# A fused transformer program on one core: first layer rebuilt up to its feed-forward

## The reference, cut to what matters

```
mod = silu(c) @ ada_w[0] + ada_b[0];  mod_c = silu(c_ctx) @ ada_w[0] + ada_b[0]
hx = rms_norm(x, norm1_g[0]) * (1 + sc1) + sh1        # and hc from ctx with mod_c
q, k, v = split(h @ attn_w_in)      # 16 query heads, 4 key and value heads of 64
q, k = rms_norm(q, q_gain), rms_norm(k, k_gain)       # per head; rope for x only
x tokens: softmax over 256 windowed keys, 256 context keys and a sink; context: 256 and a sink
x = x + g1 * (o @ attn_w_out);  hx2 = rms_norm(x, norm2_g[0]) * (1 + sc2) + sh2
x = x + g2 * conv_glu(hx2, ffn_w_up, ffn_conv_w, ffn_conv_b, ffn_w_down)
```

## Time and profile before

| | us |
|---|---|
| median of 3 executions | 2844.99 (2839.59 to 2847.72) |
| profiled execution | 2848.02, span 2846.2, mean granted clock 0.936 |
| TensorE busy over the span | 2477.9 (87%) |
| VectorE, ScalarE busy | 974.3 (34%), 775.1 (27%) |
| start to first projection | 72.5 |
| projections, then head norms to first scores | 75.4, 52 |
| attention loop with 16 modulation blocks | 197 |
| turn and output projection, entry of the feed-forward | 63, 35 |

### The profile page before, as it was taken

How to read it: one execution, slowest core, us unless ns; L and a number is a source line. 1 busy time by engine, 2 the same in 40 slices (tenths; PEclk the granted TensorE clock), 3 DMA queues, 4 the chain that set the end, 5 groups by cost and what they waited for, 6 DMA issues and landing times.

```text
span 2846.2 us, 31745 instructions
## 1 busy us (share of the span) xinstructions
PE 2477.9 (87%) x12956; PEld 1613.8 (57%) x12956; DVE 974.3 (34%) x1419; ACT 775.1 (27%) x1248; POOL 4.2 (0%) x6
## 2 busy tenths in 40 slices
PE   4939886999997997757999989799999999999995
PEld 2726653778785897654988986343333333334332
DVE  1274423334414238773654343341111111111112
ACT  2223533223314245433543453111111111111110
POOL 0000000000000000000000000000000000000000
PEclk8968997999997999887999997989999999999998
DMA  8103540442222140021555430569999999999993
GB/s 305 60 30 119 206 149 30 163 147 90 89 74 89 60 148 1 1 89 60 178 181 201 168 104 1 204 267 428 428 429 429 428 421 422 429 429 417 421 429 161
DMA packets 141897, 603.55 MB, mean 212 GB/s; under 512 B 6272, under 2 KB 51584, under 8 KB 117088
## 3 DMA queue, kind: packets, MB, share of 16 engines
q1 hardware_dynamic: 141792, 602.10, 53.5%
HBM read 601.03 MB, written 1.05 MB: 212 GB/s over the span
## 4 chain that ended last, share of the span: by engine, by line
PE 73%; DMA 10%; DVE 8%; ACT 6%; issue 2%; SPq 1%; ACTq 0%; DVEq 0%
PE bank L841 70%; DMA arena<-in_b_up 10%; ACT hT L1362 1%; PE bank L912 1%; DVE arena L2022 1%; ACT modp L1362 1%; ACT arena L1399 1%; DMA ring<-in_ada_w 1%; ACT arena L1387 1%; DVE xn L1742 1%; PE bank L873 0%; ACT modp L1338 0%; ACT hT L1376 0%; DVE modp L2012 0%; DVE xn L2011 0%
## 5 line engine op out<-in xcount | busy, mean ns | idle before, releaser
L841 PE MATMUL bank<-arena 128*64 128x512 f32 (+5 forms) x3088 | 644.2, 488 | 77.6 <-ACT arena L1692 25.7
L841 PEld LDWEIGHTS bank<-arena 128*64 128x64 f32 (+2 forms) x3088 | 340.5, 175 | 337.2 <-issue 267.5
L841 PE MATMUL bank<-ring,arena 128*64 128x512 f32 (+1 forms) x1632 | 394.9, 608 | 23.8 <-DMA arena<-in_b_up 21.0
L841 PE MATMUL bank<-hT_high,w_split 128*128 128x512 f32 (+1 forms) x1408 | 351.1, 341 | 30.4 <-issue 30.4
L841 PEld LDWEIGHTS bank<-ring,arena 128*64 128x64 f32 (+1 forms) x1632 | 141.3, 143 | 269.6 <-issue 259.7
L841 PEld LDWEIGHTS bank<-hT_high,w_split 128*128 128x128 f32 x1408 | 245.2, 192 | 60.6 <-issue 32.6
L841 PE MATMUL bank<-hT_low,w_split 128*128 128x512 f32 (+1 forms) x704 | 238.5, 339 | 0.0
L2159 DVE TENSOR_SCALAR arena<-bank 128x512 f32<-128x512 f32 x32 | 22.1, 692 | 549.5 <-PE bank L841 549.5
L841 PE MATMUL bank<-ring,hT 128*128 128x512 f32 (+1 forms) x432 | 182.6, 584 | 17.7 <-ACTq L666 17.7
L841 PEld LDWEIGHTS bank<-ring,hT 128*128 128x128 f32 x432 | 81.4, 195 | 116.6 <-issue 97.2
L841 PEld LDWEIGHTS bank<-hT_low,w_split 128*128 128x128 f32 x704 | 135.4, 192 | 15.3 <-issue 1.5
(11 more groups left out here) (307 smaller groups left out, 3418.6 us busy)
## 6 DMA issues: line engine op xcount, KB each, us to landing
ring<-in_w_gate SPq DMA_DIRECT2D x64, 2048.0 KB
arena<-in_w_down SPq DMA_DIRECT2D x64, 2048.0 KB, 15.1
ring<-in_w_up SPq DMA_DIRECT2D x32, 2048.0 KB
arena<-in_w_up SPq DMA_DIRECT2D x32, 2048.0 KB
ring<-in_ada_w SPq DMA_DIRECT2D x24, 2048.0 KB, 7.9
ring<-in_ffn_w_up SPq DMA_DIRECT2D x44, 1024.0 KB, 7.7
ring<-in_w_in SPq DMA_DIRECT2D x11, 2048.0 KB, 8.0
ring<-in_ffn_w_down SPq DMA_DIRECT2D x10, 2048.0 KB, 7.7
```

The lines of the kernel that those rows point to most:

```text
L841: return pe.matmul(o, l, r, start=start, stop=stop)
```

## The change

Stage by stage:
- Loads: tokens go first of all (after the columns); the constants without the score masks and distances behind the first unit; score masks and level masks ahead of unit 6; gate biases ahead of unit 7. The level masks land in another buffer. The output weights are streamed between modulation blocks (after the 11th and the 14th of the loop), in eight pieces each, and keep their slots; later modulation blocks use the others. The next layer's gate biases wait behind the first late modulation block.
- Norms of the first tokens into four buffers, before anything else on VectorE; turned by TensorE after the fourth block; modulated by ScalarE (chunks 0 to 3) and VectorE (4 to 7), high and low parts by tiles. Gate blocks no longer make the column form.
- All three blocks by three passes, in the order keys and values, queries 0, queries 1. Per tile ScalarE squares from PSUM, VectorE rotates from PSUM by tables that hold the gain; keys are normed there, queries keep their scale, which goes into the exponential. Key turns come before the fifth half, turns of each query block after the following half.
- Scores contract 64 rows; the two heads of a pair use the two halves of the array, and keys have no zeros. VectorE adds mask and takes the maximum in one operation for x; for the context ScalarE exponentiates straight from PSUM. VectorE scales the probabilities; they are turned by chunks of 128 keys for four heads, the values are stationary and the output comes out turned, split into high and low.
- Output projection by three passes; norm, turn, modulation and split of each tile between the tiles of its second half.

The core of the diff (indentation cut; a line of dots stands for what is left out):

```diff
+WO_AFTER = {10: 0, 13: 1}
+def out_unit(b):
+    w = a["attn_w_out"][0].rearrange("(m s j d) n -> s d m j n", m=NKV, s=2, j=2)
+    stream(("wo0", b), *[(lambda s, z=z, m=m: ring_col(s, 0, 512)[64 * z:64 * z + 64, 2 * m:2 * m + 2, :],
+                          w[z, :, m, :, b * 512:(b + 1) * 512]) for z in range(2) for m in range(NKV)])
...
+held = [] if key[0] != "ada" else [slot_of[unit_no["wo0", b]] for b in range(2)
+                                   if ("wo0", b) in names[:n] and names[n - 1][0] != "up"]
+s = [x for x in order if (x < RING - 1 or not narrow) and x not in held][0]
+s = {("hq", 0): RING - 1, ("wo0", 0): 0, ("wo0", 1): RING - 1}.get(key, s)
...
 sp.dma_start(cols[:, :], a["cols"]).then_inc(cols_landed, 16)
+tokens()
...
-if n in early:
...
+def first_turn(t):
+    turn("a0", (t,), lambda t: xn4[:, t, :], lambda t: await_next(xn_ready))
...
+def q_half(j):
+    key, z = Q_HALVES[j]
+    s = unit(key)
+    hi, lo = qw_high[j % 3], hw_low[:, s, :, 256 * z:256 * z + 256]
     parts = [(k, *p) for k in range(KC) for p in ((hi, qx_high), (hi, qx_low), (lo, qx_high))]
+    pe.wait_ge(qw_low_ready, j + 1)
     for t in ALL:
-        ps = bank((*key, t))
...
+    pe.wait_ge(qx_low_ready, t + 1)
+g = ("kv", t) if key[1] == 2 else ("q", key[1], t)
+ps = bank(g)
 for n, (k, wt, x) in enumerate(parts):
...
 if z:
-    close(m, (*key, t))
...
-release(m)
...
+elif t == NT - 1:
+    m.then_inc(q_half_used, 1)
...
+for j in range(4):
+    q_half(j)
 for t in ALL:
...
+def scores(t, g):
+    tok = slice(t * P, (t + 1) * P)
+    lo = 0 if t < XT else SEQ
+    ps = [bank(("score", t, g, r)) for r in range(4 if t < XT else 2)]
+    for r in range(4):
+        half = slice(64 * (r % 2), 64 * (r % 2) + 64)
+        o = ps[r][:, :] if t < XT else ps[r % 2][:, 256 * (r // 2):256 * (r // 2) + 256]
+        m = mm(o, qT[half, 2 * g + r // 2, tok], kT[half, g, lo:TOK], True, True)
+        if t < XT:
+            close(m, ("score", t, g, r))
+        elif r > 1:
+            close(m, ("score", t, g, r - 2))
...
+def weighted(i):
+    t, g = ATT0[i]
+    chunks = NT if t < XT else NT - XT
+    pr = P0[:, i % 2, :, :]
+    await_next(p_ready)
+    for c in range(chunks + 1):
+        if c < chunks:
+            ps = bank(("probt", t, g, c))
+            for r in range(4):
+                m = pe.transpose(ps[:, r * P:(r + 1) * P], pr[:, r, c * P:(c + 1) * P], ident)
+            close(m, ("probt", t, g, c))
+        if c:
+            await_next(pt_ready)
+            if c == 1:
+                pv = bank(("pv", t, g))
+            at = c - 1 if t < XT else c - 1 + XT
+            for s in range(2):
+                m = mm(pv[64 * s:64 * s + 64, 0:256], v0[:, at, g * HD:(g + 1) * HD],
+                       PT0[:, (c - 1) % 2, 256 * s:256 * s + 256], c == 1, c == chunks)
+    close(m, ("pv", t, g))
+for i in range(len(ATT0) + 1):
+    if i < len(ATT0):
+        scores(*ATT0[i])
+    if i:
+        ada(*ADA_BETWEEN[i - 1])
+        weighted(i - 1)
+        ada2(*ADA_BETWEEN[i - 1])
+pe.wait_ge(o_low_ready, len(ATT0))
+for b in range(2):
+    s = unit(("wo0", b))
+    for t in ALL:
+        ps = bank(("wo0", b, t))
+        for z in range(2):
+            j = 2 * b + z
+            pe.wait_ge(wo_low_ready, j + 1)
+            hi, lo = wo_high[j], hw_low[:, s, :, 256 * z:256 * z + 256]
+            parts = [(k, *p) for k in range(KC) for p in ((hi, o_high), (hi, o_low), (lo, o_high))]
+            for n, (k, wt, x) in enumerate(parts):
+                m = mm(ps[:, 256 * z:256 * z + 256], x[:, k, t * P:(t + 1) * P], wt[:, k, :], n == 0,
+                       n == len(parts) - 1)
+        close(m, ("wo0", b, t))
+        if b and t:
+            turn(("f", 0), (t - 1,), lambda t: xn[:, t % 2, :], lambda t: await_next(xn_ready))
+turn(("f", 0), (NT - 1,), lambda t: xn[:, t % 2, :], lambda t: await_next(xn_ready))
 ffn(0, NT)
...
+def enter_first():
+    for t in range(NT + 1):
+        if t < NT:
+            std(t, 1)
+        if t == 0:
+            await_next(coef_ready)
+        if t == 2:
+            weights_high(0, 0)
+        if t:
+            norm_turn(("f", 0), (t - 1,), 0, 1, split=True, stds=False)
...
+for t in ALL:
+    v = 0 if t < XT else 1
+    tok = slice(t * P, (t + 1) * P)
+    ps = take(("turn", "a0", t, 0))
+    for k in range(4):
+        do(act.activation(hT[:, k, tok], ps[:, k * P:(k + 1) * P], ACT.Identity,
+                          bias=modT[:, 0, k, v:v + 1], scale=coef[:, 0, 0, k, v:v + 1]),
+           F if k == 3 else act_step)
+    do(act.activation(qx_high[:, 0:4, tok], hT[:, 0:4, tok], ACT.Copy), qx_high_ready)
+    await_next(mod_ready)
+    do(act.activation(qx_high[:, 4:8, tok], hT[:, 4:8, tok], ACT.Copy), qx_high_ready)
+for j in range(1, 4):
+    q_half_high(j)
+squares = [0]
...
+for t in ALL:
+    take_turned(("qt", 1, t), qT[:, 4:8, t * P:(t + 1) * P], "gq")
+signal(qT_ready)
...
+for i in range(len(ATT0) + 1):
+    if i:
+        t, g = ATT0[i - 1]
+        ada(*ADA_BETWEEN[i - 1])
+        for c in range(NT if t < XT else NT - XT):
+            ps = take(("probt", t, g, c))
+            do(act.activation(PT0[:, c % 2, :], ps[:, :], ACT.Copy), F)
+            signal(pt_ready)
+        pe_past(("pv", t, g))
+        do(act.activation(o_high[:, 2 * g:2 * g + 2, t * P:(t + 1) * P],
+                          PS[group["pv", t, g] % BANKS][:, 0:256].rearrange("p (j q) -> p j q", j=2),
+                          ACT.Copy), o_high_ready)
+        if i - 1 in (13, 14):
...
+if i == len(ATT0):
+    continue
...
+for r in range(4):
...
-                o = kT[64 * z:64 * z + 64, z::2, t * P:(t + 1) * P]
-                do(act.activation(o, ps[64 * z:64 * z + 64, :, :], ACT.Copy), F if z else act_step)
-signal(qT_ready)
...
+    at = t * NH + 4 * g + r
+    do(act.activation(pr, src, ACT.Exp, bias=st[:, 4 + r:5 + r], scale=stat[:, at:at + 1],
+                      accum_out=st[:, 12 + r:13 + r]))
+if t >= XT:
+    for r in range(2):
+        signal(freed["exp"])
...
+def enter_first():
+    coefs(0, 1)
+    for t in ALL:
+        gated_add(("wo0", 0, t), 0, t, GATE[(0, 0)], tmp=region(1024, 512))
+    for t in range(NT + 1):
+        if t < NT:
+            gated_add(("wo0", 1, t), 1, t, GATE[(0, 0)], tmp=region(1024, 512))
+            rms(("f", 0), (t,))
+        if t == NT - 1:
+            signal(gates_read)
+        if t == 2:
+            weights_low(0, 0)
+        if t:
+            split_tokens(t - 1)
 def ffn(l, T):
...
+for t in ALL:
+    dve.wait_ge(x_landed if t < XT else ctx_landed, 16)
+    do(dve.tensor_tensor_reduce(out=xn4[:, t, :], in0=xr[:, t, :], in1=xr[:, t, :], scale=1.0, scalar=0.0,
+                                op0=ALU.mult, op1=ALU.add, accum_out=stat[:, t:t + 1]), ss_ready)
+for t in ALL:
+    await_next(std_ready)
+    do(dve.reciprocal(stat[:, t:t + 1], stat[:, t:t + 1]))
+    do(dve.tensor_scalar(xn4[:, t, :], xr[:, t, :], stat[:, t:t + 1], None, ALU.mult), xn_ready)
...
+v = 0 if t < XT else 1
+tok = slice(t * P, (t + 1) * P)
+ps = take(("turn", "a0", t, 1))
+for k in range(4, 8):
+    do(dve.tensor_scalar(hT[:, k, tok], ps[:, (k - 4) * P:(k - 3) * P], coef[:, 0, 0, k, v:v + 1],
+                         modT[:, 0, k, v:v + 1], ALU.mult, ALU.add), F if k == 7 else dve_step)
...
+for i in range(len(ATT0) + 1):
+    if i:
+        t, g = ATT0[i - 1]
+        st = stat[:, 64 + 32 * ((i - 1) % 2):96 + 32 * ((i - 1) % 2)]
+        n = TOK if t < XT else CTX
+        await_next(sum_ready)
+        do(TT(st[:, 12:16], st[:, 12:16], st[:, 8:12], ALU.add))
+        do(dve.reciprocal(st[:, 16:20], st[:, 12:16]))
+        for r in range(4):
+            pr = P0[:, (i - 1) % 2, r, 0:n]
+            do(dve.tensor_scalar(pr, pr, st[:, 16 + r:17 + r], None, ALU.mult),
+               p_ready if r == 3 else dve_step)
...
+if t < XT:
+    for r in range(4):
+        ps = take(("score", t, g, r))
+        do(dve.tensor_tensor_reduce(out=P0[:, i % 2, r, :], in0=ps[:, :],
+                                    in1=C("mask0", t * 512, 512), scale=1.0, scalar=-3e38,
+                                    op0=ALU.add, op1=ALU.max, accum_out=st[:, r:r + 1]), F)
...
+        t, g = ATT0[i - 1]
+        cut = (slice(None), slice(2 * g, 2 * g + 2), slice(t * P, (t + 1) * P))
+        ps = take(("pv", t, g))[:, 0:256].rearrange("p (j q) -> p j q", j=2)
+        await_next(o_high_ready)
+        do(TT(o_low[cut], ps, o_high[cut].bitcast(F32), ALU.subtract), F)
+        signal(o_low_ready)
+        ada2(*ADA_BETWEEN[i - 1])
+        if i - 1 in (14, 15):
+            out_low(i - 15)
+out_low(2)
+out_low(3)
 ffn(0, NT)
```

More of the change, by code:

```diff
@@ L326, in plan_ada, with plan_ada2 @@
             add(("adap", l, blk), "act")
-            add(("adat", l, blk), "dve")
+            plan_ada2(l, blk)
+        def plan_ada2(l, blk):
+            if blk not in G_BLOCKS:
+                add(("adat", l, blk), "dve")
             for row, v in gate_slots(l, blk):
@@ L1486, in _ @@
+            out_high(2)
+            out_high(3)
```

(33 more changed lines are left out.)

537 lines of the change are left out of this document (335 added, 202 removed).

## The result

The changed kernel takes 2749.8 us (median of 4, 2749.4 to 2752.7) against 2845.5 us in the same series: ratio 0.967, interval 0.965 to 0.969, some 96 us less. The forecast was 2722. The time lies in the range (2695 to 2765), but 28 us above the forecast and outside the 2705 to 2735 that I had given a chance of 0.55; 2749.8 is closest to the 2748 of rival (d). The profiled execution has a span of 2747.5 us, where the sum gave 2725 less the 1.8 us around it, 2723. So 24 us of the sum's own are to be found: the attention loop, from the first scores to the output projection, is 202 us long where the sum had 172, and some 6 us come back behind the first feed-forward product.

The account below looks back on a forecast made before the run. TensorE was taken to bound the loop, projections and output projection, but mostly to stand in 115 of the first 495 us. The first feed-forward product at 372, 123 us less, plus an unchanged 2351 gave 2722 on the median; range 2695 to 2765.

Parts of the forecast that it names:

- rival (d): Beside the projections, bank or buffer waits put half of the 52 us of head norms back: 2748, chance 0.05.
- rival (a): Attention loop at the low clock half of the time: +23 and +14 us, 2759; chance 0.12.
- Start: Token norms run under the loads, the turning of tokens ends last at 47.1; projections start at 47 in place of 72.5.
- Projections: Six three-pass halves of 11.66 us, the first paced by ScalarE to 58; end at 123, scores at 130.
- First pass: Start of the attention loop, from first scores until P is ready: 12.6 us.
- X passes: Attention loop, passes over x tiles: 12.15 us each, seven make 85; TensorE needs 10.8 of each.
- rival (b): Attention loop, the weighting's halves don't run side by side: +17 us, 2739; sign weighting over 6 us; chance 0.15.
- Change to context: Attention loop, the step from x passes to context passes: 10.7 us.
- Context passes: Attention loop, passes over context tiles: 8.0 us each, seven make 56.
- the ring: Attention loop's chain of ScalarE exponentials, VectorE scaling, turns and weighting, copy of output; in x passes the bound, not TensorE.
- the fear: Loop's last two modulation loads share one slot; a 9.9 us pass is enough for a load, otherwise 1 to 2 us each.
- Output projection and entry: From output projection to first feed-forward product: 29.2 us for five tiles, then 40.8 to the last low part; 302 to 372.

Follow-up runs that it names:

- the earlier trace: Profile of the kernel before the change; that profiled execution took 2848.0 us.
- the filled: Changed kernel with the modulation product issued twice in each of the seven x passes: 2746.6 us, ratio 0.9652.
- the single-row run: Changed kernel with all score products on the first 64 rows, outputs changed, so only the loop is compared: 219.5 us in place of 202.2.
- the first profile: Profiled execution of the changed kernel in its first measurement: span 2747.5 us.
- the second: Profile of the changed kernel run once more, unchanged, as a base: 2750.6 us, ratio 0.9663.
- the kernel with all three edits: Changed kernel with modulation product before context scores, entry reordered, output-weight splits behind exponentials, and second output-weight unit later: 2724.8 us, ratio 0.959.

## Why the prediction was right, and where it was off

The range held, in part by luck: the loop was 30 us longer than forecast, and what is 6 us shorter behind it was not foreseen. Two of the prediction's own signs of being wrong came up. The part behind the first feed-forward product is not 2351 us long, and the granted clock from 150 to 300 us is 0.89, under the 0.9 that stood for rival (a). What the clock cost is told below with the x and the context passes; together it is some 14 us, where (a) had 37.

**Start: the number held, by luck.** 47 forecast, 47.2 measured. The norms do run under the loads; that the tokens go ahead of the matrices is worth about 2 us at most. But "the turning is last" was wrong. TensorE's timeline after:

```profile
39.07 5.09 PE L933 MATMUL bank<-const,arena 128*128 128x128 f32 x32
...
47.25 0.36 PE L899 MATMUL bank<-qw_high,qx_high 128*128 128x256 f32 x1 [3.09 <-DVE qx_low L2185]
```

The turning ends at 44.2, since it takes 5.1 us where I had 7.9, four times the 1.97 of the earlier trace rows at the lower clock. Then TensorE waits 3.09 us for the first tile's low part, which VectorE ends at 47.0 and I had at 45.4: it has to modulate four chunks and split the first weights before it. One error hid the other.

**Projections: held**, 123 forecast and 125.6 measured. The half that was to be paced by ScalarE ends at 61.7 instead of 58: tile 3's low part comes at 58.5, 3.2 us later than in my schedule, since a tile costs 3.84 us where I had 3.3. The drain to the scores was shorter, and they start at 130.9 for 130.

**First pass: 13.7 us for 12.6.** The first maximum can start 2.3 us after the first score product, where I had 1 us; the exponentials take 0.3 us more, the maxima 0.5 less.

**X passes: right mechanism, mis-sized term.** The sum was 12.15; at full clock it is 12.4 (12.38 to 12.41 in the changed kernel, the filled and the single-row run). The exponentials are longer than I had them: they take 0.81 us at 512 columns, now that they have a scale for each row, where the earlier trace rows has 0.72, and follow at 0.94 instead of 0.85 us, 0.36 in four, against which the weighting is 0.2 shorter; 0.1 us is left open. (Only the 512-column exponentials can be compared with the earlier trace rows: those of 256 columns read PSUM now and read SBUF before.) Groups by line of the changed kernel, 128 to 335 us:

```profile
L1720 ACT ACTIVATE arena<-arena,stat 128x512 f32<-128x512 f32 x32 | 26.0, 813 | 1.0
...
L1720 ACT ACTIVATE arena<-bank,stat 128x256 f32<-128x256 f32 x32 | 18.0, 563 | 1.1
...
L2273 DVE TENSOR_SCALAR arena<-arena,stat 128x512 f32<-128x512 f32 x32 | 15.5, 486 | 1.1
```

The scaling of P, chosen at 0.49 between 0.38 and 0.69, is 0.486. The weighting took 5.3 us at full clock, so rival (b) is out; the 6.2 to 6.7 us in passes partly at the lower level are over (b)'s sign of 6 us by the clock. Four of the seven passes took 13.3 to 13.8 us, at the clock's lower level for part of them; that is 4.4 of the 6.1 us by which the seven are longer than forecast (91.2 for 85.1).

**Change to context: 15.3 us for 10.7.** In it lies a wait for a bank of 3.4 us; with the modulation product ahead of the scores it was still 14.3. The weighting is partly at the lower clock (output split 6.5 us after P, 5.4 at full clock), and scores and product, 4.6 us from 246.5, stand between the exponentials and the turning as in the context passes. I haven't taken it apart further.

**Context passes: the step that failed.** "A context pass: ... = 8.0" was a sum over the ring alone. It left out that the next scores need a bank that the exponentials free, and that TensorE's order puts scores and modulation product ahead of the turning. 78.2 us for 59.9, +18. With the product ahead a pass is 8.45 us, so the ring's own price was 0.45 short and the order was worth 2.4 us a pass, at the clock it was given. More than half of that is the clock's: scores and product took 4.3 to 5.6 us in five of the seven passes where they take 2.92 at full clock. That is some 10 us of the 18 as an estimate from these rows, and the one plain pass in which they ran at full clock took 9.35 us (295.51 to 304.86) for 10.9. I had checked TensorE's needs against the ring in x passes (10.8 of 12.15) and not in context passes, where the order of banks, not the work, is what binds. Rival (d) named "bank or buffer waits", but beside the projections.

**Loads: the fear was right, the cover too.** In the changed kernel the single slot shows no wait in the first profile and one of 4.5 us in the second, so the passes were just long enough. As soon as they are shortened, the last two cost 5.8 us. The premise had a slip: 2.1 MB each 8 us are 262 GB/s, more than the 238 of the earlier trace rows. It did no harm, since the kernel with all three edits moved 267 GB/s from 265 to 288 us.

**Output projection and entry: held**, 70 us forecast and 69.8 measured; the earlier trace rows has 57 + 35. Here the schedule held too: adds at 0, 5.8, 14.9 and 26.3 us and the last low part at 40.6, for 0, 5.8, 15, 26.3 and 40.8.

**Behind the first feed-forward product: a term I missed, for me.** 2344.6 us for 2351. The diff makes column products only for blocks that are not a gate's. The four late blocks of layer 1, which lie in the first feed-forward, are gates, so each loses eight small products. Timeline of TensorE after, the first and the last of these blocks:

```profile
426.91 1.92 PE L899 MATMUL bank<-ring,cT 128*32 128x512 f32 x16
429.96 1.12 PE L899 MATMUL bank<-modp,const 128*128 128x512 f32 x2 [1.12 <-ACTq L717]
...
504.59 1.92 PE L899 MATMUL bank<-ring,cT 128*32 128x512 f32 x16
```

The four blocks' products span 77.7 us (504.59 - 426.91). Before they spanned 82.0, as its timeline has it:

```profile
518.91 1.92 PE L841 MATMUL bank<-ring,cT 128*32 128x512 f32 x16
521.95 1.05 PE L841 MATMUL bank<-const,modp 128*128 128x2 f32 x8 [1.12 <-ACTq L666]
...
600.92 1.93 PE L841 MATMUL bank<-ring,cT 128*32 128x512 f32 x16
```

4.3 us less over three blocks, and about 1 us of small products in the fourth, are some 5.4 of the 6.4. The small products themselves are 0.92 us a block (521.95 to 522.87); the rest goes to the products right behind them, which before ran at the lower clock (1.42 us for 0.79). No run puts the small products back, so this is read from timelines and not tried. I read `if blk not in G_BLOCKS` in the diff and costed it in the loop only.

Sum of the misses up to the feed-forward: start 0.9, first pass 1.1, x passes 6.1, change 4.6, context 18.3, entry and end about 0: 31; less 6.4 behind it, 24.6, which is within rounding the 24.3 between 2723.2 and 2747.5.

## What to carry to other kernels

Where a pipeline over a few PSUM banks gets shorter passes, count the groups in a pass against the number of banks and ask what frees the bank that the next pass's first group falls on; work that needs no such bank belongs in front of it in the order, not behind. When a ring of engines becomes the bound, the engine that idles in it may be granted the lower clock, and its steps within the ring then cost double: price the ring at both levels (the modulation product took 1.92 or 3.64 us). When one wait goes, look at once for the load that the longer pass had covered.

## What the runs showed of the hardware that was not expected

More work made TensorE's own steps faster: 1.9 us of products into an idle of 2.29 us raised the granted clock from 0.87 to 1.00, and groups of four went from 1.12 to 0.65 us; in the single-row run more work did not keep the level. An exponential on ScalarE with a scale for each row takes 0.813 us for 512 columns, against 0.721 with none. A change of form on TensorE costs about 0.15 us here, 0.2 in the earlier trace rows: groups of four products follow each other at 0.58 to 0.59 us (220.09, 220.67), where four more turns of the same form add 0.43 us (eight last 1.09, four 0.66). The Trainium skill, page "TensorEngine Tiling (Array Packing)", section Key Properties, has changes of mode drain the engine; the trace agrees and gives it this price.
